# Band attention in a two-layer streaming encoder: the first two query tiles of each head pair handled in one step

## The reference

```python
qa, ka, va, qr, kr, vr, gr = project(x, norm_mix, w_in)      # 1024 -> 3584 columns
o_a = band_attention(qa, ka, va)      # 8 heads x 64: softmax(q k^T / 8 + bias) v
o_r = retention(qr, kr, vr)           # 4 heads x 128
x = x + concat([o_a, silu(gr) * norm(o_r)]) @ w_out
x = x + (silu(h @ w_gate) * (h @ w_up)) @ w_down
```

## Time and profile before

| | |
|---|---|
| median of three executions | 1430.18 us (1429.92 to 1430.29) |
| the profiled execution | 1429.94 us |
| its span, first to last instruction | 1428.2 us |
| PE busy | 1419.7 us (99%) |
| PE weight loads | 1378.6 us (97%) |
| DVE busy | 1003.7 us (70%) |
| ACT busy | 623.1 us (44%) |
| attention steps of layer 1, from the first scores to the last values | 123.3 to 231.4 us |

### The profile page before, as it was taken

How to read it: one execution, slowest core, us unless ns; L and a number is a source line. 1 busy time by engine, 2 the same in 40 slices (tenths; PEclk the granted TensorE clock), 3 DMA queues, 4 the chain that set the end, 5 groups by cost and what they waited for, 6 DMA issues and landing times.

```text
span 1428.2 us, 29091 instructions
## 1 busy us (share of the span) xinstructions
PE 1419.7 (99%) x10924; PEld 1378.6 (97%) x10924; DVE 1003.7 (70%) x1946; ACT 623.1 (44%) x1097; POOL 47.0 (3%) x89
## 2 busy tenths in 40 slices
PE   9999999999999999999999999999999999999999
PEld 8998889999999999999999988899999999999998
DVE  6348765879998359995442777567899963699832
ACT  5233444746554125553222244456465531355421
POOL 2001100100000000000010011001000000000000
PEclk9999999999999999999999999999999999999999
DMA  7324421342433323433253253115133332333332
GB/s 225 98 60 122 130 60 49 108 119 61 113 93 95 97 61 90 110 84 102 70 148 89 60 159 89 50 53 162 50 105 97 88 102 61 92 107 97 94 90 75
DMA packets 226511, 136.23 MB, mean 95 GB/s; under 512 B 4776, under 2 KB 220512, under 8 KB 226416
## 3 DMA queue, kind: packets, MB, share of 16 engines
q1 hardware_dynamic: 220240, 113.82, 28.3%
q0 software_dynamic: 5936, 20.82, 4.6%
q10 hardware_dynamic: 240, 0.32, 0.1%
HBM read 122.04 MB, written 8.18 MB: 91 GB/s over the span
## 4 chain that ended last, share of the span: by engine, by line
PE 95%; DVE 3%; issue 1%; ACT 1%; DVEq 0%; ACTq 0%
PE ps L1753 36%; PE ps L2163 34%; PE ps L1900 13%; PE ps L1950 2%; PE ps L1992 1%; PE ps L1972 1%; PE ps L1803 1%; PE ps L2243 1%; DVE sc L1260 1%; PE ps L1811 1%; PE ps L2043 0%; DVE lo_of L1053 0%; PE ps L2070 0%; PE ps L2052 0%; PE ps L1997 0%
## 5 line engine op out<-in xcount | busy, mean ns | idle before, releaser
L1753 PE MATMUL ps<-act,hi_down 128*128 128x288 f32 x1364 | 271.9, 295 | 0.0
L1753 PE MATMUL ps<-mix,hi_of 128*128 128x288 f32 x1216 | 243.8, 296 | 1.1 <-DVE lo_of L1053 0.5
L1753 PEld LDWEIGHTS ps<-act,hi_down 128*128 128x128 f32 x1364 | 218.5, 188 | 0.0
L1900 PE MATMUL ps<-mix,hi_of 128*128 128x288 f32 x1024 | 211.3, 300 | 0.0
L1753 PE MATMUL ps<-act,lo_down 128*128 128x288 f32 x682 | 201.0, 295 | 0.0
L1753 PEld LDWEIGHTS ps<-mix,hi_of 128*128 128x128 f32 x1216 | 194.4, 188 | 2.5 <-DVE lo_of L1053 1.1
L1753 PE MATMUL ps<-mix,lo_of 128*128 128x288 f32 x608 | 179.1, 295 | 0.0
L1900 PEld LDWEIGHTS ps<-mix,hi_of 128*128 128x128 f32 x1024 | 162.6, 188 | 10.4 <-issue 8.0
L1900 PE MATMUL ps<-mix,lo_of 128*128 128x288 f32 x512 | 150.8, 295 | 0.0
L901 ACT ACTIVATE hi_S<-sum_S 128x512 fp32r<-128x512 f32 x176 | 106.8, 630 | 95.6 <-DVE sum_S L1477 94.0
L2163 PE MATMUL ps<-sums_a,hi_A 128*128 128x288 f32 x704 | 142.7, 295 | 0.2
(11 more groups left out here) (272 smaller groups left out, 2706.4 us busy)
## 6 DMA issues: line engine op xcount, KB each, us to landing
raw_of<-in_w_in SPq DMA_DIRECT2D x56, 512.0 KB, 3.7
raw_down<-in_w_down SPq DMA_DIRECT2D x32, 704.0 KB, 4.7
pair_raw<-in_w_gate SPq DMA_DIRECT2D x42, 512.0 KB, 4.0
pair_raw<-in_w_up SPq DMA_DIRECT2D x42, 512.0 KB, 5.3
raw_of<-in_w_out SPq DMA_DIRECT2D x16, 512.0 KB, 4.1
mix<-att POOLq DMA_DIRECT2D x8, 576.0 KB, 5.8
strip_even<-bias_lines POOLq DMA_DIRECT2D x8, 320.0 KB, 5.9
strip_odd<-bias_lines POOLq DMA_DIRECT2D x8, 320.0 KB, 5.4
```

Of the source, the lines that this page charges most:

```text
L1753: last = nc.tensor.matmul(ps[:, bank + half, 0:HALF], weights(w, slot, nk)[:, k, :], tile[:, part, HALF * half:HALF * half + HALF], start= ...
L1900: last = nc.tensor.matmul(ps[:, half_bank(i), 0:HALF], weights(w, n % 2, KD)[:, k, :], mix[:, k, part, HALF * half:HALF * half + HALF], st ...
```

## The change

Tiles 0 and 1 of a pair of heads become one item: 128 + 256 = 384 key columns, side by side in the same PSUM banks and the same buffers. An item is now a pair and a tuple of tiles, `TILES_A`. There are 4 items per pair, 16 per layer and 18 steps, and each of the 18 has a half unit. The least values, sums and reciprocals have four columns for the merged item, not two. All waits that counted five items per pair count four.

```diff
+        TILES_A = ((0, 1), (2,), (3,), (QT,))
+        IA = len(TILES_A)
-        ITEMS_A = [(p, t) for p in range(PAIRS) for t in range(TT)]
+        ITEMS_A = [(p, tiles) for p in range(PAIRS) for tiles in TILES_A]
-        AT_A = [k for k in range(STEPS_A) if k % TT != QT - 1]
+        AT_A = list(range(STEPS_A))
+        def keys_of(tiles):
+            at = [sum(P * (u + 1) for u in tiles[0:i]) for i in range(len(tiles) + 1)]
+            return [(t, slice(at[i], at[i + 1])) for i, t in enumerate(tiles)]
...
                 def exponentials(k):
-                        for hh in range(2):
-                            e = sc[:, k % 2, hh, 0:P * (t + 1)]
+                        for i, (t, some) in enumerate(keys_of(tiles)):
+                            for hh in range(2):
+                                e, c = sc[:, k % 2, hh, some], 2 * i + hh
...
-                    if k % TT == 3 and k < NA:
-                        cache_keys(k // TT)
+                    if k % IA == IA - 1 and k < NA:
+                        cache_keys(k // IA)
...
                 def scale_probs(k):
-                    n = 2 if t < QT else 1
+                    n = 2 * len(tiles) if tiles[0] < QT else 1
...
                 for k in range(STEPS_A):
-                    late = k % TT == QT
+                    late = k % IA == IA - 1
                     if k < NA and not late:
                         scores(k)
                     if k in AT_A:
                         half_unit(PRE + AT_A.index(k))
...
-                    if k % TT == 2 and k < NA:
-                        cache_keys(k // TT)
+                    if k % IA == 2 and k < NA:
+                        cache_keys(k // IA)
```

More of the change, by code:

```diff
@@ L735, in probs_out @@
                 def probs_out(k):
-                    p, t = ITEMS_A[k]
+                    p, tiles = ITEMS_A[k]
                     eng.wait_ge(pt_ps, NA * l + k + 1)
@@ L741, in probs_out @@
                         eng.wait_ge(pv_done, NA * l + k - 1)
-                    if t < QT:
-                        w = P * (t + 1)
+                    if tiles[0] < QT:
+                        w = keys_of(tiles)[-1][1].stop
                         nc.scalar.activation(pt[:, k % 2, :, 0:w], ps[:, 4:6, 0:w], ACT.Copy).then_inc(pt_out, 1)
@@ L755, in exponentials @@
                         eng.wait_ge(sums_inv, NA * l + k - 1)
-                    if t < QT:
-                        for hh in range(2):
-                            e = sc[:, k % 2, hh, 0:P * (t + 1)]
-                            last = nc.scalar.activation(e, e, ACT.Exp, scale=-1.0, bias=least[:, k % 2, hh:hh + 1],
-                                                        accum_out=sums[:, k % 2, hh:hh + 1])
+                    if tiles[0] < QT:
+                        for i, (t, some) in enumerate(keys_of(tiles)):
+                            for hh in range(2):
+                                e, c = sc[:, k % 2, hh, some], 2 * i + hh
+                                last = nc.scalar.activation(e, e, ACT.Exp, scale=-1.0, bias=least[:, k % 2, c:c + 1],
+                                                            accum_out=sums[:, k % 2, c:c + 1])
                     else:
@@ L767, in _ @@
                 for k in range(STEPS_A):
-                    if k >= TT + 2 and (k - 2) % TT == 0:
-                        attn_out((k - 2) // TT - 1)
-                    if k % TT == 3 and k < NA:
-                        cache_keys(k // TT)
+                    if k >= IA + 2 and (k - 2) % IA == 0:
+                        attn_out((k - 2) // IA - 1)
+                    if k % IA == IA - 1 and k < NA:
+                        cache_keys(k // IA)
                     if k < NA:
@@ L1238, in add_bias @@
                 def add_bias(k):
-                    p, t = ITEMS_A[k]
+                    p, tiles = ITEMS_A[k]
                     waits = [(s_ps, NA * l + k + 1)]
-                    if t == 0:
+                    if tiles[0] == 0:
                         waits.append((strip_masked, PAIRS * l + p + 1))
@@ L1248, in add_bias @@
                     strip = strips[p % 2]
-                    for hh in range(2):
+                    for i, hh in [(i, hh) for i in range(len(tiles)) for hh in range(2)]:
+                        t, some = keys_of(tiles)[i]
                         if t < QT:
                             r, w = slice(0, P), P * (t + 1)
-                            src, bias, dst = ps[:, 2 + hh, 0:w], strip[:, hh, STRIP - w:STRIP], sc[:, k % 2, hh, 0:w]
-                            c = hh
+                            src, bias, dst = ps[:, 2 + hh, some], strip[:, hh, STRIP - w:STRIP], sc[:, k % 2, hh, some]
+                            c = 2 * i + hh
                         else:
@@ L1270, in scale_probs @@
                     dve.wait_ge(sums_inv, NA * l + k + 1)
-                    for hh in range(n):
-                        e = sc[:, k % 2, hh, 0:P * (t + 1)] if t < QT else sc_dec[:, k % 2, 0:TOK]
-                        last = nc.vector.tensor_scalar(e, e, rsum[:, k % 2, hh:hh + 1], None, ALU.mult)
+                    for c in range(n):
+                        t, some = keys_of(tiles)[c // 2]
+                        e = sc[:, k % 2, c % 2, some] if t < QT else sc_dec[:, k % 2, 0:TOK]
+                        last = nc.vector.tensor_scalar(e, e, rsum[:, k % 2, c:c + 1], None, ALU.mult)
                     last.then_inc(p_scaled, 1)
@@ L1284, in _ @@
                         half_unit(PRE + AT_A.index(k - 1))
-                    if k % TT == 1 and k < NA:
-                        decode_queries(k // TT)
+                    if k % IA == 1 and k < NA:
+                        decode_queries(k // IA)
                     if k < NA:
@@ L1940, in scores @@
                 def scores(k):
-                    p, t = ITEMS_A[k]
+                    p, tiles = ITEMS_A[k]
                     keys = qk[:, 4 + p, :]
                     waits = [(biased, NA * l + k)] if k else []
-                    if t < QT:
+                    if tiles[0] < QT:
                         for semaphore, count in waits:
                             pe.wait_ge(semaphore, count)
[L1948 to L1951, removed]
+                        for t, some in keys_of(tiles):
+                            for hh in range(2):
+                                hr = head_rows(hh)
+                                last = nc.tensor.matmul(ps[:, 2 + hh, some], q_rev[hr, p, tok(t)], keys[hr, 0:P * (t + 1)],
+                                                        start=True, stop=True)
                     else:
@@ L1968, in probs @@
                     wait_apart(pe, *waits)
-                    if t < QT:
+                    if tiles[0] < QT:
                         for hh in range(2):
-                            for s in range(t + 1):
+                            for s in range(keys_of(tiles)[-1][1].stop // P):
                                 last = nc.tensor.transpose(ps[:, 4 + hh, P * s:P * s + P], sc[:, k % 2, hh, P * s:P * s + P], ident)
@@ L1979, in values @@
                 def values(k):
-                    p, t = ITEMS_A[k]
+                    p, tiles = ITEMS_A[k]
                     waits = [(pt_out, NA * l + k + 1)]
-                    if t == 0 and p:
+                    if tiles[0] == 0 and p:
                         waits.append((ot_out, PAIRS * l + p))
-                    if t == QT:
+                    if tiles[0] == QT:
                         waits.append((vc_loaded[p % RING], 16 * (PAIRS // RING) * l + 16 * (p // RING + 1)))
                     wait_apart(pe, *waits)
[L1989 to L1993, removed]
+                    if tiles[0] < QT:
+                        for t, some in keys_of(tiles):
+                            for s in range(t + 1):
+                                for hh in range(2):
+                                    last = nc.tensor.matmul(ps[head_rows(hh), 6, tok(t)],
+                                                            va[:, s, DA * (2 * p + hh):DA * (2 * p + hh) + DA],
+                                                            pt[:, k % 2, hh, some.start + P * s:some.start + P * s + P],
+                                                            start=s == 0, stop=s == t)
                     else:
```

16 lines of the change are left out of this document (8 added, 8 removed).

## The result

The changed kernel takes 1443.68 us (median of 6 executions, 1441.74 to 1447.65) against 1430.05 (1429.66 to 1430.42) for the kernel before: ratio 1.0101, interval 1.0091 to 1.0111. It is slower by 13.6 us; 1440.7 was forecast, within 1436 to 1446. The six executions differ by 5.9 us, and two of them (1447.43 and 1447.65) lie above that range. The profiled execution took 1442.16 us, one of the shorter ones; its span is 1440.4, 12.2 more than before.

A forecast was written before the change was run, and what follows sets the result against it. PE, busy 99% of the span, was taken to bound the kernel. Per layer 6.25 us lost in waits less 1.0 saved is 5.25 net, +10.5 us for two layers: 1440.7 us, range 1436 to 1446.

The forecast's parts named there:

- The step that decides: In decode's iteration DVE does evacuation and low part behind the bias; PE's half unit waits 1.89 us, until 150.80.
- What PE would have done without the wait: Start of pairs: merged scores from 147.86 take 1.05 us, so PE would start the half unit at 148.91.
- The sign named for it: Start of pairs 2 and 3: PE gap of 1.7 to 2.0 us before half unit, released by low part.
- The saving of the joined groups: Per pair, joined scores, transposes and value products save 0.25 us of changing over (0, 0.09, 0.15); bounds 0 to 0.5.
- Step 0: ACT's token copies come behind four exponentials, so PE waits 0.3 us per layer inside the transposes; at most 1.1.
- Rival 3, the clock: Clock falls to 1.2 GHz at waits over 1.5 us, six half units at half rate: +20 us, 1460; 5%.
- Rivals 1, 2 and 4: 1: only joined groups count, 1428.2, 4%; 2: evacuation alone holds PE, 1431, 4%; 4: late low part delays transfer, 1449, 9%.
- The cover of tile 2's iteration: In other steps the low part is ready about 0.75 us (layer start) or 1.6 (later pairs) before PE's need.

The follow-up runs named there:

- e1: Changed kernel with the half unit's evacuation and low part put ahead of decode's bias on DVE; 1425.51 us, ratio 0.9966.
- e2: Changed kernel with only the low part put ahead of decode's bias, the evacuation still behind it; 1429.27 us, ratio 0.9993.
- e5: Kernel before, nothing merged, half unit moved from tile 1's steps (except in the tail) to tile 3's; 1453.89 us, ratio 1.0156.
- e4: Changed kernel run again without edits, on the same chip as the others; 1442.53 us, ratio 1.0094.
- e3: Changed kernel with dummy matmuls (4, 4, 1 and 3 per layer) on PE where it waits; 1439.74 us, ratio 1.0069.
- e9: Changed kernel with about half of e3's dummy matmuls (2, 2, 0 and 2 per layer); 1439.64 us, ratio 1.0067.
- e8: e1's kernel with ACT's first token tile copy between tile 0's and tile 1's exponentials in step 0; 1423.87 us, ratio 0.9957.
- e6: e1's kernel with ACT's first token tile copy ahead of all four exponentials of step 0; 1427.19 us.

## Why the prediction was right

- **The step that decides**, DVE's evacuation and low part behind decode's bias, was right in place, releaser and time: the half unit started at 150.80, as worked out. e1 shows that it is the cause of the loss, e2 that the low part ends the wait, e5 that it needs no merging.
- **What PE would have done without the wait** was mis-sized. I took the merged scores as 1.05 us, the sum of the single groups. They take 0.86, which makes the wait 0.19 longer. They also started 0.11 earlier than in the kernel before (147.75, not 147.86), while the evacuation on DVE did not. So the wait was 2.19, not 1.89 (in the other places 0.76 for 0.46, 1.80 for 1.71). The sign named for it, a gap of 1.7 to 2.0 us, was missed by that much (2.13).
- **The saving of the joined groups** was mis-sized the other way: 0.25 per pair was taken, with a bound of 0.5, and it is 24.85 - 24.17 = 0.68, outside the bound. Scores 0.19; transposes 0.09 and values 0.15 as worked out; the rest is in groups that are not merged but have another neighbour now. `cache_keys` takes 0.41 where a half unit follows (141.32 to 141.73 in e1), and took 0.58 ahead of scores (138.51 to 139.09); tile 2's six transposes take 0.74 behind a half unit (139.77 to 140.51) and took 0.81 behind scores (140.15 to 140.96). I had looked only at the groups that the edit touches.
- **Step 0** was right in place and releaser: 0.3 was forecast, and the list has 0.35 of idle time. By distances the step lost 0.50 per layer.
- **The number came out partly by luck.** These errors nearly cancelled: 9.4 us of net waits where 10.5 was forecast. The lower clock, put at nothing in the forecast, brought it back up: 2.9 in the profiled execution, some 4 at the median (13.6 - 9.4). With two more of the six executions like the two longest, the median would have been above the range.
- **Rival 3, the clock**, was given 5% as a case by itself. In fact it comes on top of the forecast and in part: two of six long gaps in one profile, five in another, 1.4 to 1.5 us each instead of 3.3, since the clock is back before the half unit is through. What stood against it, that the gaps are shorter than the half unit behind them, did not keep the clock up. What decides behind which gaps it falls stays open.
- The Trainium skill (TensorE: Matmul & The Clock Gate, section "HAM oscillation — how this bites in real kernels"), which the prediction weighed, says that the array falls back to half its clock in idle gaps between bursts and that the burst behind runs cold. The trace agrees in kind (granted clock 0.72 and 0.69 in the stretches behind two gaps of 2.13 us), but here it was not every gap, and not the whole half unit.
- Rivals 1, 2 and 4 did not happen. The cover of tile 2's iteration held: PE has no wait for a low part at the even steps k % 4 = 2.

## What to carry to other kernels

An item in an in-order queue that waits for a late partner holds everything behind it. When steps are made fewer, look at which pieces of the other work slide behind such an item, and put the work that is ready ahead of it: two to five instructions moved per pair of heads were worth 17 to 18 us, and the merge with them in place 5. Where two independent chains share an engine, work out the slack between each product and its next reader, in both orders. And a gap on a saturated matrix engine can cost more than its length, with a spread in the times as its mark.

## What the hardware showed that was not expected

- The granted clock fell behind some gaps of 1.7 to 2.1 us and not behind others: 2 of 6 in one execution and 5 of 6 in another, with gaps equal to 0.1 us. In e5, with gaps up to 2.6 us, it fell behind 4 of 6 in one execution and behind none in another. The fall came as late as 1.3 us into the half unit (e4), and each cost 1.4 to 1.5 us. Filled with matmuls of no use, or cut to 1.1 us, the same waits left the clock full (e3, e9) and the spread fell from 6 us to 1.4 or less. One execution of the kernel before, which has no such gap in its attention, had a mean granted clock of 0.949 and took 1433.03 us; all its others had 0.999 or 1.000. It has no trace, and its cause is open.
- The scores of two tiles, four matmuls over 64 rows (two of 128 and two of 256 columns), take 0.86 us in one group, and 0.42 + 0.63 = 1.05 in two groups. The time to the next group depends on the neighbours: 0.41 or 0.58 us for the same four transposes of `cache_keys`.
- A table load of 1.28 us on ACT stands ahead of the first exponential of the attention. At 115.65, while ACT had nothing else to do, it cost nothing (e8). With one copy put ahead of it, the load came at 128.55, and PE waited 1.22 us for what followed from it (e6).
